# Where the dense blocks' operands stand in on-chip memory: two strips and a wider padded buffer in a two-layer attention and mLSTM trunk

## The reference

```
for layer in range(DEPTH):                                  # DEPTH = 2
    hnorm = rms_norm(x, mixer_norm[layer])
    x = x + (attention_mixer if layer == 0 else mlstm_mixer)(hnorm, ...)
    x = x + sq_relu_mlp(rms_norm(x, mlp_norm[layer]), mlp_w_in[layer], mlp_w_out[layer])

def sq_relu_mlp(x, w1, w2):                                 # w1 1024 x 4096, w2 4096 x 1024
    hid = jax.nn.relu(x @ w1)
    return (hid * hid) @ w2
```

## The kernel before, in words

| buffer | first block | second block |
|---|---|---|
| `hid_hi` | 17792, 384 | 17536, 128 |
| `hid_lo` | 50560, 384 | 50304, 128 |
| `hT_hi` | 122848, 480 | 126944, 480 |
| `hT_lo` | 155616, 480 | 159712, 480 |
| `w_hi` | 104928, 480 | 101504, 128 |
| `w_lo` | 113120, 480 | 109696, 128 |

## Time and profile before

### The profile page before, as it was taken

How to read it: one execution, slowest core, us unless ns; L and a number is a source line. 1 busy time by engine, 2 the same in 40 slices (tenths; PEclk the granted TensorE clock), 3 DMA queues, 4 the chain that set the end, 5 groups by cost and what they waited for, 6 DMA issues and landing times. The chain is left out here.

```text
span 3354.6 us, 48256 instructions
## 1 busy us (share of the span) xinstructions
PE 3188.1 (95%) x17466; PEld 2671.8 (80%) x17466; DVE 1337.2 (40%) x3725; ACT 1107.3 (33%) x3002; POOL 824.2 (25%) x598
## 2 busy tenths in 40 slices
PE   4999999999999995999999999899877999999999
PEld 3888888888888884788888888678665788888887
DVE  6446565555546554431313133531064422313131
ACT  4555555555555553210202112111254211111110
POOL 3333333333233311122222222112211212222121
PEclk8999999999999996999999999999898999999999
DMA  2112121121212104111111111111201111111112
GB/s 98 37 38 63 40 61 52 50 56 46 54 44 62 51 16 164 38 51 51 44 51 49 46 51 45 36 47 45 81 32 51 45 50 51 44 51 45 50 49 78
DMA packets 89904, 177.01 MB, mean 53 GB/s; under 512 B 25515, under 2 KB 55870, under 8 KB 89662
## 3 DMA queue, kind: packets, MB, share of 16 engines
q1 hardware_dynamic: 87358, 169.63, 15.9%
q10 hardware_dynamic: 2304, 4.20, 0.3%
HBM read 160.67 MB, written 13.12 MB: 52 GB/s over the span
## 5 line engine op out<-in xcount | busy, mean ns | idle before, releaser
L69 PE MATMUL ps_qk<-w_hi,attn_hT_hi 128*128 128x256 f32 x1536 | 438.1, 285 | 22.7 <-DVE attn_hT_lo L213 9.7
L915 POOL TENSOR_TENSOR first_w_lo<-first_raw,first_w_hi 128x1024 fp32r<-128x1024 f32 x96 | 231.7, 2413 | 901.6 <-ACT first_w_hi L911 901.6
L70 PE MATMUL ps_qk<-w_lo,attn_hT_hi 128*128 128x256 f32 x1536 | 436.7, 284 | 0.0
L71 PE MATMUL ps_qk<-w_hi,attn_hT_lo 128*128 128x256 f32 x1536 | 436.6, 284 | 0.0
L857 POOL TENSOR_TENSOR w_lo<-raw,w_hi 128x384 fp32r<-128x384 f32 x192 | 193.7, 1010 | 660.1 <-ACT w_hi L602 660.1
L915 POOL TENSOR_TENSOR second_w_lo<-second_raw,second_w_hi 128x1024 fp32r<-128x1024 f32 x72 | 172.2, 2392 | 630.1 <-ACT second_w_hi L911 630.1
L69 PEld LDWEIGHTS ps_qk<-w_hi,attn_hT_hi 128*128 128x128 f32 x1536 | 294.8, 192 | 27.0 <-issue 12.7
L70 PEld LDWEIGHTS ps_qk<-w_lo,attn_hT_hi 128*128 128x128 f32 x1536 | 295.6, 192 | 0.4
L71 PEld LDWEIGHTS ps_qk<-w_hi,attn_hT_lo 128*128 128x128 f32 x1536 | 295.7, 193 | 0.0
L69 PE MATMUL first_ps<-first_hid_hi,first_w_hi 128*128 128x512 f32 x640 | 255.6, 399 | 32.4 <-DVE first_hid_lo L1239 32.4
L635 ACT ACTIVATE prob<-ps_s,neg_max 128x128 f32<-128x128 f32 (+1 forms) x384 | 156.3, 412 | 362.3 <-DVE neg_max L726 362.3
(11 more groups left out here) (276 smaller groups left out, 6850.3 us busy)
## 6 DMA issues: line engine op xcount, KB each, us to landing
raw<-in_wqkv SPq DMA_DIRECT2D x192, 192.0 KB, 2.3
first_raw<-in_w SPq DMA_DIRECT2D x64, 512.0 KB, 3.4
second_raw<-in_w SPq DMA_DIRECT2D x64, 512.0 KB, 3.4
w_bc<-share_dram SPq DMA_DIRECT2D x48, 256.0 KB, 4.4
first_raw<-in_vo_pieces SPq DMA_DIRECT2D x16, 512.0 KB, 3.5
bias<-bias_dram SPq DMA_DIRECT2D x16, 256.0 KB, 3.5
yT_dram<-o_g SPq DMA_DIRECT2D x8, 512.0 KB, 3.2
first_raw<-in_attn_wo SPq DMA_DIRECT2D x8, 512.0 KB, 3.5
```

Source lines behind the costliest of these rows:

```text
L69: pe.matmul(out, a_hi, b_hi, start=first, stop=False)
L70: pe.matmul(out, a_hi, b_lo, start=False, stop=False)
L71: return pe.matmul(out, a_lo, b_hi, start=False, stop=last)
L915: pool.tensor_tensor(self.lo[:, n % 2, :], self.raw[:, n % self.RAW, :], self.hi[:, n % 2, :].bitcast(F32), ALU.subtract).then_inc(self.lo ...
```

## The change

Three allocations change; no instruction is added, taken away or moved. All five engines' lists of instructions are the same before and after, in number and in order, but for the line numbers, which grow by 2 from line 931 on and by 3 or 4 in `trunk`.

```
 CONV = 4
+LINE_PAD = 24
+PAD_COLS = SEQ + 56
...
-        self.padded = sb("padded", [P, 2, CONV - 1 + SEQ])
+        self.padded = sb("padded", [P, 2, PAD_COLS])
...
         ident = ctx.enter_context(nc.sbuf_tensor("ident", [P, P], F32))
+        ctx.enter_context(nc.sbuf_tensor("line_pad", [P, LINE_PAD], F32, side="right"))
         total = ctx.enter_context(nc.sbuf_tensor("total", [P, SEQ], F32, side="right"))
...
         rstd = ctx.enter_context(nc.sbuf_tensor("second_rstd", [P, SEQ], F32, side="right"))
+        ctx.enter_context(nc.sbuf_tensor("second_lead", [P, 64], F32))
         hid = hidden_buffers(nc, ctx, "second")
```

## The result

| | before | changed |
|---|---|---|
| median of 4 runs each | 3357.15 us (3356.14 to 3360.37) | 3332.22 us (3331.03 to 3333.34) |
| ratio | | 0.9924, 95% interval 0.9911 to 0.9938 |
| span of the profiled execution | 3354.6 us | 3331.6 us |

The change takes 24.9 us off, 0.74%. The forecast was 3334 us, in a range of 3328 to 3343.

The account below looks back on a forecast made before the run. The prediction took TensorE, with a matmul under way in 95% of the span, as the bound. First block 14.3 plus second block 9.9 made 24.2 us, off the median 3358.1: forecast 3334 us, range 3328 to 3343.

Parts of the forecast that it names:

- equal residues give 226.8 ns, whichever the residue: Dense blocks: moving and stationary operands at equal residues modulo 512 start matmuls 226.8 ns apart, also at 384.
- w2 stage of the first block: First block, moving `hid`: operands become equal, 2.89 us gained per stage of 384 matmuls, four stages 11.56 us.
- w1 stage of the second block: Second block, moving `hT`: operands become equal, 2.55 us gained for each of four stages, 10.20 us.
- The out stage: First block, a fifth stage with the w2 operands: 360 of 384 matmuls counted as gaining, 2.71 us.
- the wait behind the means: Second block: TensorE waits for a chain on VectorE, ScalarE and GpSimd; 0.32 us of gain only lengthens it.
- The stages that the forecast counted: First block's four w2 stages and out stage, 14.3 us, and second block's four w1 stages, 9.9 us.
- The covers: Dense blocks: VectorE, ScalarE and GpSimd mostly wait for TensorE, so nothing becomes late; moved buffers there cost nothing.
- One pair alone healing: Rival, chance 0.08: only one block's slow pair speeds up, residue being part of the condition; 3343.8 or 3348.2 us.
- No effect: Rival, chance 0.04: the two rates go along with the addresses only by accident; 3358 us.
- The slow rival, absolute place: Rival, chance 0.04: where an operand stands counts, so everything at 384 runs at 234.3 ns; 3394 us.

Follow-up runs that it names:

- p2: The changed kernel with `padded` at 1027 columns again, so the first block's weights at 480, `hid` and `hT` at 384: 3365.88 us.
- p3: The changed kernel without `line_pad`, so both blocks' `hT` at 480 and everything else at 384: 3360.8 us.
- p4: The changed kernel with only low parts moved, first block's `hT_lo` to 288 and second block's `w_lo` to 480: 3364.2 us.

## Why the prediction was right

**The place of the gain** was right: only the first block's `hid` stages and the second block's `hT` stages changed. The step "equal residues give 226.8 ns, whichever the residue" held; 384 was no other case.

**The sizes.** A w2 stage of the first block gained 89.97 - 87.04 = 2.93 us where 2.89 was forecast, a w1 stage of the second block 89.62 - 87.04 = 2.58 where 2.55 was. The four w2 stages thus gave 11.7 us of the forecast 11.56. The out stage got 3.1 us shorter (95.66 to 92.57), but TensorE started it 1.2 us later behind the last of the attention, and from the attention's end to the first w1 piece the gain was 1.9 us (126.93 to 125.04) instead of 2.7. In the second block the three undisturbed w1 stages gave 7.7 us. The first one, for which the forecast gives 2.55 - 0.32 = 2.2 us, gave only 0.6 (94.48 to 93.84): 0.3 us went into the wait behind the means, and the window of that stage shows a granted clock of 0.98, where before it had 1.00 (first the changed kernel, then before):

```profile
2636.70:2718.40 81.70, 78.57 (x339) 0.98 0.14 46
```

```profile
2651.60:2733.50 81.90, 79.04 (x338) 1.00 0.14 45
```

The first block's first w1 stage had the opposite luck, 0.96 before and 0.98 after, and came out 1.2 us shorter without any change of rate. These are the few us that the forecast's range allowed for the clock. In the profiled executions the span fell by 23.0 us. The stages that the forecast counted gave 21.9 of the 24.2 us. Some 2.5 us more came from stages whose rate did not change: this 1.2 us, 0.7 in the second block's out stage, and 0.6 between the first q and k piece and the second block. The attention took 1.8 us back, where the forecast had it keep its time to 1 us; its scatter is larger than that. The medians fell by 24.9 us. That this is within 0.7 us of the forecast is partly luck; that the two kinds of stage gained 2.93 and 2.58 us is not.

**The covers** held: VectorE, ScalarE and GpSimd have the same busy time, and of TensorE's waits in the dense blocks only the two named grew.

**The rivals.** One pair alone healing didn't occur. "No effect" is out, by the result and by p2 and p3. This is also where the measurement goes against a page: the Trainium skill, "TensorE: Matmul & The Clock Gate" (What happens when you issue a matmul, step 1), says that loading the next tile's weights takes no read bandwidth from the running matmul, and here the place of the weights alone, in p2 against the changed kernel, moves the spacing from 226.7 to 234.3 ns. That it is the load that does this is argued below, and not shown. The slow rival, absolute place, is out by four common residues with the same 226.7 or 226.8 ns.

**What the forecast had not seen.** It took the residue modulo 512 from the change's own terms. From the trace of before it could not be told from a smaller modulus: with 0, 352 and 416 alone, 64, 128 and 256 all fit (32 does not, since 352 and 416 are multiples of it). The number came out right because equality modulo 512 includes equality modulo 256.

## What to carry to other kernels

When TensorE is the bound and each matmul loads its own stationary tile, compare the distance between starts of stages that have the same instructions; if they differ at the same clock, look at the addresses of the two operands. Give moving and stationary buffers of back-to-back 512-column float32r products the same residue modulo 256 bytes, low and high parts alike, and move all of them together: one pad without its partner gained nothing, and in one of the two cases cost 8 us more than no pad at all. Don't carry the best distance over to another shape of matmul, but measure it there; a strip of a few dozen bytes is a cheap experiment, and it also means that an unrelated change of a buffer's size can move a kernel's time by 1%: the fourteen kernels here have the same instructions and took 3311.6 to 3373.2 us.

## What the runs showed of the hardware that I had not expected

The weight load beside a matmul starts with it. The timeline of the changed kernel with both sequences:

```profile
2850.31 0.39 PE L69 MATMUL second_ps<-second_hT_hi,second_w_hi 128*128 128x512 f32 x1
2850.32 0.19 PEld L70 LDWEIGHTS second_ps<-second_hT_lo,second_w_hi 128*128 128x128 f32 x1
...
2850.54 0.39 PE L70 MATMUL second_ps<-second_hT_lo,second_w_hi 128*128 128x512 f32 x1
2850.54 0.19 PEld L71 LDWEIGHTS second_ps<-second_hT_hi,second_w_lo 128*128 128x128 f32 x1
```

The next tile's load begins within 0.01 us of the running matmul, and is there for 0.19 of the 0.23 us. Both read a row of adjacent values in each partition, the load 512 bytes and the matmul 2048. That would fit a memory whose parts repeat every 256 bytes, in which two readers get into each other's way at some distances. The period, the grades (0, 2.2, 5.6, 6.6, 7.6 ns) and the independence from the absolute place are shown for these 512-column products; the reading as a conflict between the two is only argued, since no run took the loads away, and p4 does not fit its simplest form. Steps below 32 bytes weren't tried.

The attention's best strip (192 bytes) and the dense blocks' alignment make 3311.6 us in one execution, 45 us or 1.3% under the kernel before, with two strips in the dense blocks, one in the attention, and no other edit.
